# The scan's preparation stands inside the input projection, and the residual rows wait in a DRAM tensor

## What is computed

```python
def rwkv_prep(r, k, v, wd, ad, w0, w2, a0, a2, k_k, k_a):
    w_log = -softplus(-(w0 + einsum("bldr,drc->bldc", tanh(wd), w2))) - 0.5
    decay = exp(-exp(w_log))
    a = sigmoid(a0 + einsum("bldr,drc->bldc", ad, a2))      # rate, one per direction d
    kk = heads(k * k_k); kk = kk / max(sqrt(sum(kk * kk, -1)), 1e-12)
    k_dir = heads(k[:, :, None, :] * (1 + (a - 1) * k_a))
    b_vec = kk[:, :, None] * heads(a)
...
# scan: S = S * decay + (S @ -kk) b_vec^T + v k_dir^T ; y = S r
...
pl = split(hl @ w_in, SPLIT_IDX)       # r, k, v, wd, ad, gd, cb, cc, ch
out = concat([rwkv_readout(...), cb * short_conv(cc * ch, conv_w)]) @ w_out
xl = layer_norm(DN_ALPHA * xl + ml[2] * out, ln1_g, ln1_b)
```

## Time and profile before

| what | value |
|---|---|
| median of 3 runs | 2729.55 us (2723.61 to 2729.87) |
| profiled execution | 2728.8 us, its span 2727.1 us |
| mean granted TensorE clock | 0.960 |
| PE busy | 2483.1 us, 91% |
| DVE, ACT, POOL busy | 780.7, 636.2, 589.7 us |
| projection of layer 0, first to last matmul | about 71 to 239 us |
| preparation of layer 0 | 239.2 to 294.8 us |
| scan of layer 0 | 294.8 to 492.1 us |
| projection, preparation, scan of layer 1 | about 1141 to 1253, 1253 to 1302, 1302 to 1482 us |
| DMA in the busiest slices | 320 to 375 GB/s |

### The profile page before, as it was taken

The page is one execution under the profiler, slowest core; times in us unless marked ns, Lnnn a source line. Parts: engine busy times, 40 slices in busy tenths (PEclk is TensorE's granted clock), DMA queues, the critical chain, the costliest instruction groups (busy, mean ns, idle before and its releaser), DMA issues.

```text
span 2727.1 us, 63124 instructions
## 1 busy us (share of the span) xinstructions
PE 2483.1 (91%) x28806; PEld 1550.7 (57%) x28806; DVE 780.7 (29%) x1430; ACT 636.2 (23%) x971; POOL 589.7 (22%) x361
## 2 busy tenths in 40 slices
PE   5997799779999999696898799999999999999997
PEld 3674577457777778484676644444444444344444
DVE  2125666542222223517565410100000010101002
ACT  1232554332222222343654200000000000000002
POOL 4332543323344434245442200000000000000000
PEclk8999899889999999898999899999999999999998
DMA  7451000213434442130002489999898989898990
GB/s 249 152 173 47 6 4 4 93 62 138 155 139 156 147 160 93 47 101 8 7 4 65 194 320 352 355 354 358 342 368 324 384 329 381 330 370 335 375 359 29
DMA packets 197130, 536.49 MB, mean 197 GB/s; under 512 B 6640, under 2 KB 80640, under 8 KB 191744
## 3 DMA queue, kind: packets, MB, share of 16 engines
q1 hardware_dynamic: 193728, 528.50, 52.5%
q10 hardware_dynamic: 3136, 3.85, 0.4%
HBM read 531.28 MB, written 1.05 MB: 195 GB/s over the span
## 4 chain that ended last, share of the span: by engine, by line
PE 47%; DVE 2%; issue 1%; ACT 1%; POOL 0%; DMA 0%; POOLq 0%; DVEq 0%; ACTq 0%; SPq 0%
PE bank L719 24%; PE bank L722 12%; PE bank L692 1%; PE bank L750 1%; PE bank L707 1%; PE bank L710 1%; PE bank L1717 1%; PE bank L1713 1%; PE bank L1728 1%; PE bank L1690 0%; POOL w_lo L306 0%; PE bank L1613 0%; PE bank L1699 0%; ACT arena L1065 0%; DVE arena L1487 0%
## 5 line engine op out<-in xcount | busy, mean ns | idle before, releaser
L719 PE MATMUL bank<-arena 128*32 128x512 f32 (+1 forms) x6624 | 814.1, 559 | 20.9 <-issue 19.6
L722 PE MATMUL bank<-arena 128*32 128x256 f32 (+1 forms) x6624 | 488.7, 362 | 0.0
L306 POOL TENSOR_TENSOR w_lo<-arena,w_hi 128x2048 fp32r<-128x2048 f32 x78 | 354.6, 4547 | 591.1 <-ACT w_hi L300 591.1
L722 PEld LDWEIGHTS bank<-arena 128*32 128x32 f32 x6624 | 220.0, 110 | 435.6 <-issue 407.5
L316 PE MATMUL bank<-h_hi,w_hi 128*128 128x512 f32 (+1 forms) x1008 | 388.1, 385 | 49.7 <-DVE h_lo L1221 40.9
L318 PE MATMUL bank<-h_hi,w_lo 128*128 128x512 f32 (+1 forms) x1008 | 376.3, 373 | 0.0
L317 PE MATMUL bank<-h_lo,w_hi 128*128 128x512 f32 (+1 forms) x1008 | 373.8, 371 | 0.0
L719 PEld LDWEIGHTS bank<-arena 128*32 128x32 f32 x6624 | 210.4, 110 | 144.5 <-issue 36.2
L316 PEld LDWEIGHTS bank<-h_hi,w_hi 128*128 128x128 f32 x1008 | 192.7, 191 | 116.7 <-issue 61.2
L634 DVE TENSOR_TENSOR arena<-arena,bank 128x768 f32<-128x768 f32 (+2 forms) x45 | 31.3, 713 | 696.1 <-ACT arena L509 696.1
L318 PEld LDWEIGHTS bank<-h_hi,w_lo 128*128 128x128 f32 x1008 | 192.1, 191 | 35.8
(11 more groups left out here) (263 smaller groups left out, 2591.3 us busy)
## 6 DMA issues: line engine op xcount, KB each, us to landing
arena<-in_moe_w_dram SPq DMA_DIRECT2D x189, 2048.0 KB, 9.5
arena<-in_w_mod_dram SPq DMA_DIRECT2D x48, 1024.0 KB, 5.0
arena<-in_ffn_w_dram SPq DMA_DIRECT2D x42, 1024.0 KB, 7.1
arena<-in_w_in_dram SPq DMA_DIRECT2D x26, 1024.0 KB, 5.5
arena<-in_w_out_dram SPq DMA_DIRECT2D x8, 1024.0 KB, 9.4
arena<-in_ctx_dram ACTq DMA_DIRECT2D x1, 1024.0 KB, 11.3
arena<-in_x_dram ACTq DMA_DIRECT2D x1, 1024.0 KB, 13.3
arena<-in_w_in_dram SPq DMA_DIRECT2D x2, 512.0 KB, 5.1
```

The source lines that it names most:

```text
L306: pool.tensor_tensor(lo, slot_view(splits[i][0]), hi, ALU.subtract).then_inc(sem("w_lo"), 1)
L719: mm(bank[b][64 * h + 32 * c:64 * h + 32 * c + 32, 0:n // 2], xa[:, 32 * c:32 * c + 32], w[:, n // 2 * h:n // 2 * (h + 1)], start=first, s ...
L722: ins = mm(bank[b + 1][blk(q), 0:n // 4], xb, w[:, n // 4 * q:n // 4 * (q + 1)], start=first, stop=last)
```

## The change

- **Decays.** Decay matmul i (0 to 7) stands after column tile 15+i, in bank 6, and waits for the sigmoid before it. Its sigmoid goes into `mrow` in ScalarE's round for tile 16+i, its four scans and the rest up to qm and qt in VectorE's. The two Exps of qm and qt stand in ScalarE's round for tile 25.
- **Convolutions.** Convolution j stands in VectorE's round after U of j+1 was due, the last one behind the forward rates.
- **Rates.** The 8 rate matmuls come first after the projection, in banks 4 to 6. The four forward ones go through `tmp`; the four backward ones into a tensor of their own, RATE1, from which VectorE makes its two products each inside scan stage 0. GpSimd's key products are cut in two groups of four, the second behind stage 0's masks.
- **Values.** V is turned into banks 0 to 3, and copied to VTK after the first Exps of the staging.
- **Small matrices.** `w2z` is zeroed before the projection's weights are cut, and loaded in ScalarE's round for tile 4.
- **Residual.** Q takes over X's place in the arena. So X (2 MB) is written to a DRAM tensor `x_store` in ScalarE's round for tile 2, the first scans wait for that, and it is read back when the scan's last output is out; the residual sums after the output projection wait for the read.

The core of the diff:

```diff
+        x_store = nc.dram_tensor("x_store", [P, KD, T], fp32).ap()
...
-        VTK = area(o + 2048, NT, NP, P)
+        VTK = area(o_hb, NT, NP, P)
+        RATE1 = area(o_hb + 2048, NP, T)
...
# ScalarE, in its round for column tile ct
+                    if ct == 2:
+                        act.wait_ge(sem("xa"), 2 * l + 1)
+                        act.dma_start(x_store, X).then_inc(sem("x_out"), 16)
...
+                    if 0 <= ct - 16 < 2 * NP:
+                        i = ct - 16
+                        act.wait_ge(sem("lora_mm"), 4 * NP * l + i + 1)
+                        wait(act, "lora_use", 4 * NP * l + i)
+                        act.activation(mrow[:], bank[6][:], ACT.Sigmoid, bias=pcol(l, "w0", i)).then_inc(sem("lora_sig"), 1)
...
                 act.wait_ge(sem("y_done"), YTOT[l])
+                act.wait_ge(sem("x_out"), 16 * (l + 1))
+                act.dma_start(X, x_store).then_inc(sem("x_in"), 16)
...
# VectorE, in its round for column tile ct
+                    if j > 0:
+                        conv(j - 1)
...
+                        wait(dve, "x_out", 16 * (l + 1))
+                        dve.wait_ge(sem("lora_sig"), 4 * NP * l + i + 1)
+                        for t in range(NT):
+                            ins = nc.vector.tensor_tensor_scan(Q[:, d, j, t, 1:P + 1], ones_t,
+                                                               mrow[:, t * P:(t + 1) * P], 0.0, ALU.mult, ALU.add)
+                        ins.then_inc(sem("lora_use"), 1)
...
                 for j in range(NP):
-                    m, ctok = MIX[:, NP + j], LTOK(l)
...
+                    rates(0, j, tmp[:, j % 2])
+                conv(NP - 1)
...
+                    if st == 0:
+                        rates(1, 0, RATE1[:, 0])
+                        rates(1, 1, RATE1[:, 1])
...
# TensorE, after column tile ct
+                    if 0 <= ct - 15 < 2 * NP:
+                        i = ct - 15
+                        pe.wait_ge(sem("lora_load"), 64 * (l + 1))
+                        if l == 0 and i == 0:
+                            pe.wait_ge(sem("mod_cols"), 2)
+                        wait(pe, "lora_sig", 4 * NP * l + i)
+                        mm(bank[6][:], w2z[:, 0, i // NP, i % NP * P:(i % NP + 1) * P], WD, start=True, stop=True) \
+                            .then_inc(sem("lora_mm"), 1)
```

160 lines of the change are left out of this document (81 added, 79 removed).

## The result

The changed kernel takes 2754.73 us in the median of 4 runs (2751.99 to 2758.79), against 2726.96 us in the median of 4 runs (2723.61 to 2729.87) for the kernel before on the same chip: ratio 1.010, 95% interval 1.0084 to 1.0115. It is slower by about 27 us. The profiled execution has a span of 2750.2 us, 23.1 more than before, at a granted clock of 0.958 (0.960 before).

The account below looks back on a forecast made before the run. VectorE was taken to bound the stretches before each scan, TensorE the projection. Layer 0's terms summed to +5 and layer 1's to +16, together +21 on 2728.8, giving 2750 us; range 2739 to 2762, wider 2728 to 2765.

Parts of the forecast that it names:

- each of its signs: Tiles 16 to 23 some 20 us longer, shorter stretches, a 7 us convolution op, later level 2, later output weights.
- Stalls: Projection: TensorE waits for ScalarE's sigmoid after tiles 16 to 22; with the decay matmuls +20.5 and +21.6 us by layer.
- The handshake of layer 1: Layer 1's projection: TensorE's waits for copy, weight cut, table load and sigmoid after tiles 16 to 22, 15.7 us.
- The stretch: From the projection's last tile to the first scan matmul: 26 and 29.5 us left, so -29.5 and -19.7.
- Rates in stage 0: Scan stage 0: eight more VectorE ops a layer for the backward rates, before levels 2 and 3, +6 us a layer.
- Store and reload: Residual rows to DRAM and back: store +1 us in layer 0, 0 in layer 1; reload +4 us a layer.
- The bound that I had set for this case: Reload at the scan's end: 5.7 us more if the residual's long rows win over the first output weights.
- Clock: TensorE drops to 1.2 GHz after some of 14 new projection gaps, 1.7 us each; a third taken, +3 and +4 us.
- (a): Near nothing: stalls as priced, rates in stage 0 at bare price, reload hidden, no clock loss; about 2730 us, chance 0.15.
- (b): Faster: preparation shrinks to its dependent chain, stretches +21 and +17; about 2712 us, chance 0.07 together with the no-stall rival.
- (c): Much slower: TensorE's clock stays lower through most of the projection's rest; 2767 us, chance 0.12.
- Rival (d): Projection: no stall, ScalarE being a tile ahead; 2721 us, chance 0.07 together with the rival of a shrunken preparation.

Follow-up runs that it names:

- s1_sigmoid_early: Changed kernel with ScalarE computing decay sigmoid i in its round for tile 15+i instead of 16+i; 2721.75 us, ratio 0.9965 to the kernel before.
- r1_reload_later: Changed kernel with the residual rows asked for after the first output weight cut instead of before it; 2742.23 us, ratio 1.0051 to the kernel before.
- g1_rates_later: Changed kernel with backward rates moved behind levels 1 and 2 of scan stages 1 and 2, key products behind those stages; 2750.27 us, ratio 1.0073.
- g2_rates_in_gaps: Changed kernel with backward rates in VectorE's gaps in scan stages 0 and 1, key products behind stages 1 and 2; 2745.53 us, ratio 1.0074.
- p1_pieces: Changed kernel with GpSimd's subtraction of the middle value as eight instructions instead of one; 2750.38 us, ratio 1.0082 to the kernel before.
- c2_combined_half: Changed kernel with sigmoids and decay sums a round earlier, later reload, rates in gaps, subtraction's backward half in pieces in the scan; its total time is not in the text.
- b1_store_reload_only: Kernel before with only the residual rows' store after tile 2 and reload at the scan's end added; 2741.36 us, ratio 1.0039 to the kernel before.

## Why the prediction was right, point by point

Forecast 2750 (2728 to 2765), slower with 0.78; measured 2754.7. The mechanism was the one named, and each of its signs showed up, the first output weights at 10.9 and 10.6 us after the scans' ends where 8 to 10 was said.

1. **Stalls: right, layer 0 to within 10%.** Layer 0 by tile, predicted 1.65, 2.1, 1.3, 2.4, 1.3, 2.1, 2.6, in sum 13.4; measured 1.92, 2.16, 1.36, 2.72, 1.36, 2.16, 2.78, in sum 14.5. Layer 1 was put at 15.7 + 2.6 = 18.3 and measured 16.7. The table loads in it are 1.28 each, with the sigmoid starting at their end, as the sum had them: behind tile 22, with a load, TensorE stands 2.78 us, behind tile 18, without one, 1.36, with nothing else different; the 2.66 that the prediction sets beside the row would not fit in the 1.42 between them. The handshake of layer 1, 15.7, was 1.0 short; the 2.6 were not there. They were for two sigmoids that wait for blocked sums. In the changed kernel the stall itself gives the sums the time to end, and this wait only came up once the stalls were gone, in s1_sigmoid_early. The matmuls were priced at 0.89 each, 7.1 a layer, and cost 5.4 in layer 0 as s1_sigmoid_early shows. The total in the projection was 24.45 and 26.3 us against 23.5 and 25.6, clock included.
2. **The stretch: right in its chain, some 2 us too long.** Predicted 26 and 29.5, measured 24.4 and 27.4. The subtraction ends 6.0 us before tile 26's end in layer 0 (257.58 against 263.62; said: 6) and 4.0 after in layer 1 (1285.99 against 1282.02; said: 4.4). The third product ends at +5.3 and +10.3 (said: 5.5 and 10.9). The two microseconds are in the rates (7.1 for four in place of 8) and in factors and memset (1.6 in place of 2.5).
3. **Rates in stage 0: +6 a layer said, +5.4 and +6.9 measured,** of it 4.4 before level 2 in layer 0 (said: 4.0).
4. **Store and reload: mis-sized.** +4 said for the reload, 5.6 and 5.4 measured, and +1 for the store, 0 measured. The step that failed is "where two queues were busy together their shares were about equal". At 10 to 20 us they were; in the first 6 us of the reload q10 had 73.6% and q1 4.5%. The bound that I had set for this case (5.7, the reload ahead of the weights) is what happened. What differs between the two places is the packet: at 10 to 20 us both queues' packets are about 1 KB; in the reload 1.56 MB went in 95 packets, about 16 KB each, and q1's are about 1 KB (80 for 0.08 MB). The Trainium skill (DMA: Bandwidth & Descriptors, "Queues, rings and completion order") has each engine take turns between queues packet by packet; if its packet is what the profile counts as one, the bytes then divide as the packet sizes, and the two rows agree in direction, 95 packets against 80. No run changed the packets' size, so this cause is argued and not shown; that the order decides is shown.
5. **Clock: 3 + 4 said, 3.4 + 5.1 measured.** I took a third of 14 gaps, and 5 fell. That the size came out is in part luck: r1_reload_later, g1_rates_later, g2_rates_in_gaps and p1_pieces have the same seven gaps in layer 0, to 0.01 us, and in their profiles the clock fell behind 3, 3, 3 and 5 of them, where it was 2 here (3 in layer 1 in all five). What decides it these runs do not show; at 1.71 us each it moves the time by up to 5 us.

The sum was +21 us, the profiles differ by 19.5 at the first expert weights and 23.1 at the end, the timing by 27.8. The range 2739 to 2762 is narrower than the ends that it names: with clock, reload and stage 0 all at their lower or all at their upper ends the sum gives 2730 or 2767. Rivals (a), (b) and (c) each needed their terms at an end; only the reload was near one, its upper, and the store at its lower, 0. Rival (d) was the one worth having: "ScalarE being a tile ahead" is what s1_sigmoid_early writes into the code. I had put it at 2721, and it measured 2721.75. That agreement is in part luck, since my number was 29 us under the forecast and the edit gave 37; it took off the stalls and not the clock's loss that goes with them.

## What to carry to other kernels

When work is put into a loop that two engines walk tile by tile, compare the round in which each side does it: a result that is made and wanted in the round of the same tile is a full handshake, and one line that makes it a round earlier gave 37 us here. Price a moved step in each place it goes through, because position alone decided most of what two of these terms cost: a rate in a gap of VectorE against one beside it, a reload behind the first weight against one ahead of it. And where two engines exclude each other, moving or splitting the long instruction mostly moved the time to another place here: half of the subtraction put into the scan took 3.4 us off layer 1's stretch and came with 2.65 us more in its scan.

## What the runs showed of the hardware

- **A VectorE op with one SBUF input waits for GpSimd too.** In c2_combined_half a multiply of 512 columns by a scalar, 0.49 us alone, took 3.15, to 0.3 us behind the end of GpSimd's subtraction, while a product with one input in PSUM just ahead of it took its usual 0.67. VectorE's and GpSimd's timelines of that kernel:

```profile
230.48 0.67 DVE L1314 TENSOR_TENSOR arena<-arena,bank 128x512 f32<-128x512 f32 x1
231.19 3.15 DVE L1294 TENSOR_SCALAR arena<-arena,par 128x512 f32<-128x512 f32 x1
```

```profile
229.96 4.10 POOL L891 TENSOR_TENSOR arena<-arena,qm 128x2064 f32<-128x2064 f32 x1
```

  The prediction had spoken of ops with two SBUF inputs alone. The Trainium skill (SBUF — State Buffer, "Who interferes with whom") does list such multiplies among the ops that can take the shared port pair, under conditions on their operands, and this row agrees. The forward rates' pitch of 2.0 fits it: in the kernel after, the first op of a rate starts at 269.93, 0.44 us into GpSimd's key product (269.49, 1.64 us), and lasts 1.49 in place of 0.54.
- **A split GpSimd instruction takes longer beside VectorE.** The subtraction took 7.27 us as one, and its eight pieces 9.84 from the first start to the last end in layer 0, each 1.08 to 1.49 over both layers, with VectorE's ops between them. How much of the 2.6 us is waiting and how much the splitting itself is not shown.
- **The same code in the scan runs at either clock.** In b1_store_reload_only, whose scan is that of the kernel before, the granted clock in layer 0's scan stayed at 0.50 from 295 to 317 us; in the kernel before it had come up by 300. Both start after VectorE's stretch of some 50 us. b1's scan was 3.3 us longer. In the kernel after, the low level lasts from 295.3 to 312.4, between the rates. So a part of its 5.4 us may be the clock and not the rates; g2_rates_in_gaps, which moved the rates, had 7 us of it in place of 17. Over the whole scans, layer 0 and layer 1, the time at the low level is 15.1 and 4.3 us before, 30.0 and 11.3 in b1, 24.4 and 16.8 in the kernel after, 14.1 and 7.1 in g2. An estimate from these: b1's 14.9 and 7.0 us more came with scans 3.3 and 1.3 us longer, so the 9.3 and 12.4 us more of the kernel after would be worth some 2 us a layer, and the rates the rest of its 5.4 and 6.9. Which was first, the gap or the clock, is left open.
